# Two weight chunks of expert 1 fetched during the output projection, and 32 KB runs from expert 4 on instead of from expert 7

## The chip, the core and the metric

The kernel runs on one NeuronCore of one Trainium2 chip. The metric is the device time of one execution, in microseconds; the kernel before was run three times and gave 1279.51, 1280.52 and 1283.01 us, median 1280.52 us. Five engines take part: TensorE (PE) multiplies matrices, VectorE (DVE), ScalarE (ACT) and GpSimd (POOL) do element-wise work, and SyncE (SP) issues the transfers from HBM into the on-chip memory (SBUF), which 16 DMA engines then carry.

## The reference: what is computed

One decoder layer over 256 tokens of width 1024, all in float32. The input is layer-normalised, then a token mixer runs: one combined projection `x @ w_in` feeds a gated delta-rule branch, a short-convolution branch and a cross-attention branch; each is projected by `w_br` and gated, the three are summed, and `merged @ w_o` is the output projection. After a second layer norm comes a mixture of experts:

```python
logits = x @ w_router + b_router          # 32 experts, each token takes its top 4
gu = xb @ w_gate_up[e] + b_gate_up[e]     # 1024 -> 2048 for the tokens of expert e
gate, up = split(gu); gate = min(gate, 7); up = clip(up, -7, 7)
h = (up + 1.0) * (gate * sigmoid(gate * 1.702))
y += (h @ w_down[e] + b_down[e]) * weight # 1024 -> 1024
```

and a last layer norm. Every expert has 8 MB of `w_gate_up` and 4 MB of `w_down`, so the 32 experts together read 384 MB (402.7 million bytes), each byte once.

## The kernel before, in words

**Mixer.** The mixer's weights come in 21 pieces of 2 MB through three buffers (`raw`). Each is split into a high and a low part (ACT casts, DVE or POOL subtracts), and PE makes three products per matmul from them. The last two pieces are the two halves of `w_o`. The left operands live in `src_hi`/`src_lo` (branch outputs) and `act_hi`/`act_lo` (the normalised input, later the merged sum). PE needs `src` until the last branch projection `("br", 0, 7)`, and `act` until the last output projection `("wo", 1, 1)`. DVE's eight `sum` steps (line 1623) follow the last branch projections; `wait_sums(eng, KD)` waits for the last of them.

**Experts.** An item is one expert with up to 64 of its tokens; there are 32 items here. Its weights are six chunks of 2 MB: chunks 0 to 3 hold `w_gate_up`, chunks 4 and 5 `w_down`. This text numbers the chunks of all experts in one row: chunk m is part m % 6 of expert m // 6, so expert 1 has chunks 6 to 11, expert 4 begins with chunk 24 and expert 7 with chunk 42. PE works through them in order. After the quarters q = 0, 1, 2 of gate/up it raises `chunks_used`, after q = 3 `gu_done`, after the first half of the down projection `chunks_used`, after the second `down_done`.

**The ring.** The chunks land in a ring of ten slots of 2 MB, and an eleventh slot, `once`, takes chunk 10 only. Chunk m has slot m for m < 10, slot (m - 1) % 10 for the chunks after chunk 10, and slot m % 10 from `PAIRED_FROM` on (`slot_of`). At that place one slot is skipped. SP issues the transfers in order. Before it issues one, it waits until PE has used up what lies in the slot (`chunk_spent`). All chunks are on one DMA queue of SP. The memory of the ring's slots 0 to 5 is free early (slots 0 to 2 once the mixer's weights have been split), the slots 6 to 9 (`late_slots`) lie over the mixer's `act`/`src` tensors, and in slot 9 lies also `x1T`, the transposed input of the router, which PE needs until the four `residual` steps have raised `x1_added`. In `once` lie the router's tables, free when `onehots` has been raised.

**Single and paired transfers.** Before `PAIRED_FROM` each chunk is a transfer of its own, 128 rows with one run of 16 KB each (`chunk_dma`, line 792), and waits for the chunk that used its slot: chunk m waits for chunk m - 10 (m - 11 up to m = 20). From `PAIRED_FROM` on the four gate/up chunks of an expert come as two transfers of 4 MB, with runs of 32 KB into two neighbouring slots (`pair_dma`, line 797), and the waits are other ones: the pair (m, m + 1) waits for chunk m - 8, a down chunk m for chunk m - 9.

Of the kernel before, what the change touches and what calls it, by code (L numbers as in the profile page):

```python
# [29 lines left out]
F32R = mybir.dt.float32r  # L30
# [7 lines left out]
P = 128  # L38
D = 1024
T = 256  # L40
NT = T // P
KD = D // P
# [17 lines left out]
EC = 6  # L60
RING = 10
ROUND = 5
# [106 lines left out]
def hybrid_layer(nc, x, mem, ln0_g, ln0_b, w_in, conv_qkv, conv_mix, a_log, dt_bias, gdn_norm,  # L169
                 w_mem_kv, w_br, w_o, ln1_g, ln1_b, w_router, b_router, w_gate_up, b_gate_up,  # L170
                 w_down, b_down, ln2_g, ln2_b, out):
    with ExitStack() as ctx:
        def sb(name, shape, dt=F32, scope=ctx):
            return scope.enter_context(nc.sbuf_tensor(name, shape, dt))

        def sem(name):
            return ctx.enter_context(nc.semaphore(name))
# [56 lines left out]
        early = ExitStack()  # L234
# [32 lines left out]
        probs = e.at(o_mem, H, 2 * T).rearrange("p h (t m) -> p h t m", t=NT)  # L267
        gates = e.at(o_mem, KD, T)
        GATED = e.used
        act_hi, act_lo = (sb(n, [P, KD, T], F32R, early) for n in ("act_hi", "act_lo"))  # L270
        src_hi, src_lo = (sb(n, [P, KD, T], F32R, early) for n in ("src_hi", "src_lo"))
        s_max, s_neg, s_sum, s_rec = (e.new(H, NT) for _ in range(4))
        w_ab, ab_rows = e.at(o_qkv + R, KD, 2 * H), e.at(o_eb, T)
        chunk_ident = sb("chunk_ident", [P, CHUNK], scope=early)
# [11 lines left out]
        l = Space(sb("late", [P, LATE]), LATE)  # L286
# [14 lines left out]
        cnt, ext, ext2 = l.new(1), l.new(1), l.new(1)  # L301
        assert l.used <= GATED, (l.used, GATED)
        scratch = scratch.rearrange("p a b -> p (a b)")
# [5 lines left out]
        weightT4 = sig1[:, T:T + P]  # L309
        late_slots = [l.new(SLOT) for _ in range(4)]  # L310
        both = l.used - 4 * SLOT
        x1T = l.at(l.used - KD * T, KD, T)


        assert l.used <= LATE - SLOT, (l.used, LATE)
        l.used = LATE - SLOT
        once_o = l.used; once = l.new(SLOT)
        o = once_o
        logits, el, mask = (l.at(o + NT * NE * n, NT, NE) for n in range(3))
        o += 3 * NT * NE  # L320
        top_v, top_f, top_e = (l.at(o + NT * 8 * n, NT, 8) for n in range(3))
# [35 lines left out]
        x1_added = sem("x1_added")  # L357
# [16 lines left out]
        onehots, gathered, tokens_in = sem("onehots"), sem("gathered"), sem("tokens_in")  # L374
# [11 lines left out]
        def bank_of(u):  # L386
            return unit_at[u] % BANKS

        def turn_of(u):
            return unit_at[u] // BANKS + 1  # L390
# [358 lines left out]
        def wait_sums(eng, count):  # L749

            for c in range(max(0, count - BANKS), count):
                eng.wait_ge(bank_free[bank_of(("br", 0, c))], turn_of(("br", 0, c)))
# [25 lines left out]
        def raw_spent(sp, n):  # L778

            for who in split_lo:  # L780
                sp.wait_ge(split_lo[who], lo_count(4 * n + 3, who))


        def chunk_dma(sp, c, gu, dn, dst, landed):


            if c < 4:
                src = gu[4 * P * (c // 2):4 * P * (c // 2 + 1), :].rearrange("(p k) n -> p (k n)", k=4)
                src = src[:, SLOT * (c % 2):SLOT * (c % 2 + 1)]
            else:  # L790
                src = dn[4 * P * (c - 4):4 * P * (c - 3), :].rearrange("(p k) n -> p (k n)", k=4)
            sp.dma_start(dst, src).then_inc(landed, 16)

        def pair_dma(sp, c, gu, m):

            src = gu[4 * P * (c // 2):4 * P * (c // 2 + 1), :].rearrange("(p k) n -> p (k n)", k=4)
            sp.dma_start(PAIRS[slot_of(m) // 2], src).then_inc(ring_place(m)[1], 16)
# [4 lines left out]
        def slot_of(m):  # L802


            return m % RING if m < RING or m >= PAIRED_FROM else RING if m == RING else (m - 1) % RING

        def signals(m):

            return m < PAIRED_FROM or m >= (NE - 1) * EC or m % 2 == 0 or m % EC == EC - 1

        def ring_place(m, rounds=0):

            r = slot_of(m)
            fill = MIXER_FILLS[r] + sum(signals(n) for n in range(m + 1) if slot_of(n) == r)
            per_round = sum(signals(n) for n in range(2 * ROUND * EC, 3 * ROUND * EC) if slot_of(n) == r)
            return RING_SLOTS[r], RING_IN[r], (rounds * per_round + fill) * 16
# [8 lines left out]
        def chunk_spent(eng, m, items=0):  # L825

            i, c = items + m // EC, m % EC
            if c == 3:
                eng.wait_ge(gu_done, i + 1)
            elif c == 5:  # L830
                eng.wait_ge(down_done, i + 1)
            else:
                eng.wait_ge(chunks_used, 4 * i + (c + 1 if c < 3 else 4))

        PAIRED_FROM = (2 + ROUND) * EC
        EARLY_CHUNKS = {15: 3, 16: 4, 17: 5}

        block = ctx.enter_context(nc.Block())  # L840
# [2 lines left out]
        def _(sp):  # L843
# [20 lines left out]
            for n in range(2, N_MIX):  # L864
                slot_dma(sp, n)
                if n in EARLY_CHUNKS:

                    sp.wait_ge(ya_ready, 1)
                    c = EARLY_CHUNKS[n]
# [4 lines left out]
            for r in range(4):  # L874
                n, c = r // 2, r % 2
                sp.dma_start(bgu[NE * r:NE * (r + 1), :], b_gate_up[0, :, FF * n + 512 * c:FF * n + 512 * (c + 1)]).then_inc(ebias_in, 16)
            for n, m in enumerate((ln1_g, ln1_b)):
                for c in range(2):
                    sp.dma_start(gb_cols[:, n, 4 * c:4 * c + 4],
                                 m[0, 4 * P * c:4 * P * (c + 1)].rearrange("(p k) -> p k", k=4)).then_inc(lnp_in[1], 16)  # L880
            for c in range(RAW):
                raw_spent(sp, N_MIX - RAW + (c - N_MIX) % RAW)
                chunk_dma(sp, c, w_gate_up[0, 0], w_down[0, 0], *ring_place(c)[0:2])
            sp.wait_ge(bank_full[bank_of(("wo", 1, 1))], turn_of(("wo", 1, 1)))
            for c in range(EC):
                if EC + c == RING - 1:

                    sp.wait_ge(x1_added, 2 * NT)
                if EC + c == RING:
                    sp.wait_ge(onehots, 1)  # L890
                if EC + c > RING:
                    chunk_spent(sp, EC + c - RING - 1)
                chunk_dma(sp, c, w_gate_up[0, 1], w_down[0, 1], *ring_place(EC + c)[0:2])
            for ex in range(2, 2 + ROUND):
                for c in range(EC):
                    m = EC * ex + c
                    chunk_spent(sp, m - RING - (m <= 2 * RING))
                    chunk_dma(sp, c, w_gate_up[0, ex], w_down[0, ex], *ring_place(m)[0:2])
                if ex == 3:
                    chunk_spent(sp, RING)  # L900
                    for r in range(4):
                        sp.dma_start(bdown[NE * r:NE * (r + 1), :], b_down[0, :, 512 * (r % 2):512 * (r % 2 + 1)]).then_inc(ebias_in, 16)
            with sp.Fori(1, ROUNDS - 1) as j:
                for u in range(ROUND):
                    ex = ROUND * j + (2 + u)
                    gu = w_gate_up[0, bass.ds(ex, 1), :, :].rearrange("e d f -> (e d) f")
                    dn = w_down[0, bass.ds(ex, 1), :, :].rearrange("e d f -> (e d) f")
                    for c in range(0, 4, 2):
                        m = EC * (2 + ROUND + u) + c
                        chunk_spent(sp, m + 2 - RING, ROUND * (j - 1))  # L910
                        pair_dma(sp, c, gu, m)
                    for c in range(4, EC):
                        m = EC * (2 + ROUND + u) + c
# [3 lines left out]
            for ex in range(2 + ROUND * (ROUNDS - 1), NE):  # L917
                paired = ex < NE - 1
                for c in range(EC):
                    m = EC * ex + c  # L920
# [13 lines left out]
            with sp.If_ne(sp.to_reg(n_items), NE):  # L934
                with sp.Fori(NE, n_items) as i:
                    ex = sp.value_load(ids_i[0:1, bass.ds(i, 1)], min_val=0, max_val=NE - 1)
# [255 lines left out]
        def _(pe):  # L1192
# [3 lines left out]
            def piece(q):  # L1196

                pe.wait_ge(split_lo[lo_engine(q)], lo_count(q))
                _, hi, lo = piece_views(q)
                return hi, lo  # L1200
# [716 lines left out]
```

## Time and profile before

| | |
|---|---|
| median of 3 runs | 1280.52 us (1279.51 to 1283.01) |
| time of the profiled execution | 1282.62 us |
| its span | 1280.9 us |
| share of the span: PE / DVE / ACT / POOL busy | 95% / 31% / 19% / 11% |
| HBM read | 451.64 MB |
| experts: first gate/up matmul to last down matmul | 361.16 us to 1266.8 us |

The profile shows one execution. PE's busy share says little by itself, since matmuls are pipelined and their recorded ends are modelled; who is waited for is read from the chain of waits and from the issue and landing times of the transfers. "To landing" is the time from a transfer's issue on SP until all of it is there, so it includes the time it stands in the queue behind earlier ones.

### The profile page before, as it was taken

Reading aid. Unit: us, or ns where it says so; the run is one execution under the profiler, and the core shown is the slowest. Engines: PE = TensorE matmul, PEld = TensorE weight load, DVE = VectorE, ACT = ScalarE, POOL = GpSimd, SP = SyncE. Lnnn points to the kernel's source line nnn. Section 1 sums busy time; section 2 is a strip of 40 time slices with the busy share of each in tenths; the row PEclk is TensorE's granted clock in tenths of the full one; section 3 lists DMA queues with packets and bytes.
Section 4 is the critical chain, followed back from the end, with each engine's and each line's share of the span. In section 5 each row is a group of like instructions: output and inputs, shape, how many; then the busy total and the mean of one; then the engine's idle time right before and its main releaser. Section 6 shows DMA issues by size and latency. Waiting matters only on the chain.

```text
span 1280.9 us, 16880 instructions
## 1 busy us (share of the span) xinstructions
PE 1217.3 (95%) x7135; PEld 616.2 (48%) x7135; DVE 392.6 (31%) x784; ACT 241.3 (19%) x387; POOL 146.1 (11%) x106
## 2 busy tenths in 40 slices
PE   6989999999999999999999999999999999999996
PEld 5789999998843333333333333333333333333332
DVE  5375553434521221221221221221112222122224
ACT  4355345444310000000000000000000000000001
POOL 8223432455200000000000000000000000000000
PEclk9899999999999999999999999999999999999998
DMA  9533323475799999999999999999999999999994
GB/s 299 200 133 132 115 85 128 171 304 196 277 401 420 398 427 426 420 431 428 430 435 428 431 430 427 433 431 427 430 430 430 432 432 426 429 432 430 426 425 179
DMA packets 49512, 453.62 MB, mean 354 GB/s; under 512 B 6110, under 2 KB 10283, under 8 KB 31019
## 3 DMA queue, kind: packets, MB, share of 16 engines
q1 hardware_dynamic: 49450, 452.71, 85.2%
q8 instruction: 51, 0.84, 0.3%
q14 instruction: 11, 0.08, 0.0%
HBM read 451.64 MB, written 1.05 MB: 353 GB/s over the span
## 4 chain that ended last, share of the span: by engine, by line
PE 72%; DMA 19%; DVE 3%; ACT 2%; POOL 2%; issue 1%; SPq 0%; ACTq 0%; DVEq 0%; POOLq 0%
PE bank L1386 27%; DMA late<-in_w_gate_up_dram 19%; PE bank L1459 13%; PE bank L1203 6%; PE bank L1204 5%; PE bank L1205 5%; PE bank L1472 4%; PE bank L1357 3%; PE bank L1372 2%; PE bank L1447 1%; ACT late L1175 1%; POOL w_lo L758 1%; ACT w_hi L1079 1%; PE bank L1467 1%; PE bank L559 1%
## 5 line engine op out<-in xcount | busy, mean ns | idle before, releaser
L1386 PE MATMUL bank<-late 128*64 128x512 f32 x1632 | 368.1, 598 | 10.4 <-DMA late<-in_w_gate_up_dram 10.2
L1386 PEld LDWEIGHTS bank<-late 128*64 128x64 f32 x1632 | 112.6, 137 | 242.2 <-issue 217.6
L1459 PE MATMUL bank<-late 128*64 128x512 f32 x816 | 182.5, 599 | 5.3 <-ACT late L1175 5.3
L1203 PE MATMUL bank<-act_hi,w_hi 128*128 128x256 f32 x448 | 130.1, 290 | 6.9 <-POOL w_lo L758 3.7
L1204 PE MATMUL bank<-act_lo,w_hi 128*128 128x256 f32 x448 | 126.5, 282 | 0.0
L1205 PE MATMUL bank<-act_hi,w_lo 128*128 128x256 f32 x448 | 126.4, 282 | 0.0
L1802 DVE TENSOR_SCALAR late<-bank 128x512 f32<-128x512 f32 x32 | 22.1, 692 | 306.2 <-PE bank L1386 306.1
L1459 PEld LDWEIGHTS bank<-late 128*64 128x64 f32 x816 | 56.9, 138 | 112.8 <-issue 104.4
L1386 PE MATMUL bank<-raw,late 128*64 128x512 f32 x416 | 93.4, 596 | 3.2 <-DMA raw<-in_w_gate_up_dram 3.2
L758 POOL TENSOR_TENSOR w_lo<-raw,w_hi 128x1024 fp32r<-128x1024 f32 x33 | 82.0, 2487 | 117.0 <-ACT w_hi L1079 116.9
L1203 PEld LDWEIGHTS bank<-act_hi,w_hi 128*128 128x128 f32 x448 | 85.1, 190 | 9.3 <-issue 4.1
L1204 PEld LDWEIGHTS bank<-act_lo,w_hi 128*128 128x128 f32 x448 | 85.2, 190 | 0.1
L1205 PEld LDWEIGHTS bank<-act_hi,w_lo 128*128 128x128 f32 x448 | 85.1, 190 | 0.0
L1168 ACT COPY late<-bank 128x512 f32<-128x512 f32 x33 | 19.3, 586 | 331.6 <-PE bank L1357 331.6
L1813 DVE COPY late<-bank 64x512 f32<-64x512 f32 x32 | 22.2, 694 | 189.9 <-PE bank L1459 189.9
L1079 ACT CAST w_hi<-raw 128x1024 fp32r<-128x1024 f32 x56 | 58.5, 1047 | 80.2 <-issue 48.3
L1472 PE MATMUL bank<-late 64*128 64x512 f32 x256 | 63.6, 615 | 1.0 <-DVE late L1873 1.0
L1357 PE MATMUL bank<-hx,late 128*64 128x512 f32 x264 | 62.3, 593 | 0.0
L1177 ACT COPY late<-bank 64x512 f32<-64x512 f32 x32 | 18.5, 579 | 232.0 <-PE bank L1459 232.0
L1386 PEld LDWEIGHTS bank<-raw,late 128*64 128x64 f32 x416 | 28.6, 137 | 62.5 <-issue 55.8
L1173 ACT ACTIVATE late<-late 128x512 f32<-128x512 f32 x32 | 20.1, 629 | 180.4 <-DVE late L1802 180.4
L1817 DVE COPY late<-bank 128x256 f32<-128x256 f32 x31 | 13.2, 425 | 130.3 <-PE bank L1467 130.3
(320 smaller groups left out, 1247.6 us busy)
## 6 DMA issues: line engine op xcount, KB each, us to landing
late<-in_w_gate_up_dram SPq DMA_DIRECT2D x38, 4096.0 KB, 31.8
late<-in_w_down_dram SPq DMA_DIRECT2D x51, 2048.0 KB, 30.6
late<-in_w_gate_up_dram SPq DMA_DIRECT2D x26, 2048.0 KB, 13.5
raw<-in_w_gate_up_dram SPq DMA_DIRECT2D x10, 4096.0 KB, 31.7
raw<-in_w_down_dram SPq DMA_DIRECT2D x13, 2048.0 KB, 32.9
raw<-in_w_in_dram SPq DMA_DIRECT2D x8, 2048.0 KB, 7.8
early<-in_w_in_dram SPq DMA_DIRECT2D x6, 2048.0 KB, 7.6
raw<-in_w_gate_up_dram SPq DMA_DIRECT2D x6, 2048.0 KB, 10.6
```

The lines of the kernel that those rows point to most:

```text
L758: ops.tensor_tensor(lo, src, as_f32(hi), ALU.subtract).then_inc(split_lo[who], 1)
L1079: a.copy(hi, src).then_inc(split_hi, 1)
L1203: mm(o, l_hi, r_hi, start=start, stop=False)
L1204: mm(o, l_hi, r_lo, start=False, stop=False)
L1205: return mm(o, l_lo, r_hi, start=False, stop=stop)
L1357: ins = mm(ps[0][64 * c:64 * c + 64, :], onehot[:, t, :], hx[:, t, 512 * c:512 * (c + 1)], start=(t == 0), stop=(t == NT - 1))
L1372: mm(ps[1 + n][64 * c:64 * c + 64, :], e_row[rows, :], bgu[rows, :], start=True, stop=False)
L1386: ins = mm(bk[64 * c:64 * c + 64, :], x_slotT[:, k % 4, 64 * (k // 4):64 * (k // 4) + 64], w[:, kk, at + 512 * c:at + 512 * (c + 1)], star ...
L1459: ins = mm(ps[3][64 * c:64 * c + 64, :], hidT[:, kk, 64 * q:64 * q + 64], w[:, kk, c * 512:(c + 1) * 512], start=(q == 0 and kk == 0), sto ...
L1472: ins = mm(ps[4 + 2 * t + c][:, :], scatter[64 * c:64 * c + 64, t * P:(t + 1) * P], y_tok[64 * c:64 * c + 64, :], start=False, stop=True, ...
L1802: d.tensor_scalar(gate1, ps[1][:, :], LIMIT, None, ALU.min).then_inc(gate_cut, 1)
L1813: d.tensor_copy(y_tok[64:128, :], ps[3][64:128, :]).then_inc(y_copied, 1)
```

## The change

Four edits. (1) `src_hi`/`src_lo` and `act_hi`/`act_lo` change places in memory, so that the ring's slots 6 and 7 lie over `src` alone. (2) `x1T` moves from slot 9 into `once`. (3) The chunks 6 and 7 are issued between the chunks 0 and 1, after the wait for the mixer's last sum. The chunks 8 and 9 stay behind the last output projection (9 no longer waits for `x1_added`), and chunk 10 waits for `x1_added` and `onehots`. (4) `PAIRED_FROM` goes from 42 to 24.

```diff
+        src_hi, src_lo = (sb(n, [P, KD, T], F32R, early) for n in ("src_hi", "src_lo"))
         act_hi, act_lo = (sb(n, [P, KD, T], F32R, early) for n in ("act_hi", "act_lo"))
-        src_hi, src_lo = (sb(n, [P, KD, T], F32R, early) for n in ("src_hi", "src_lo"))
...
-        x1T = l.at(l.used - KD * T, KD, T)
...
+        x1T = l.at(once_o + 1024, KD, T)
...
-        PAIRED_FROM = (2 + ROUND) * EC
+        PAIRED_FROM = 4 * EC
...
+            def second(c):
+                chunk_dma(sp, c, w_gate_up[0, 1], w_down[0, 1], *ring_place(EC + c)[0:2])
+
             for c in range(RAW):
                 raw_spent(sp, N_MIX - RAW + (c - N_MIX) % RAW)
                 chunk_dma(sp, c, w_gate_up[0, 0], w_down[0, 0], *ring_place(c)[0:2])
+                if c == 0:
+
+                    wait_sums(sp, KD)
+                    second(0)
+                    second(1)
             sp.wait_ge(bank_full[bank_of(("wo", 1, 1))], turn_of(("wo", 1, 1)))
-            for c in range(EC):
-                if EC + c == RING - 1:
-
-                    sp.wait_ge(x1_added, 2 * NT)
-                if EC + c == RING:
-                    sp.wait_ge(onehots, 1)
-                if EC + c > RING:
-                    chunk_spent(sp, EC + c - RING - 1)
-                chunk_dma(sp, c, w_gate_up[0, 1], w_down[0, 1], *ring_place(EC + c)[0:2])
+            second(2)
+            second(3)
+            sp.wait_ge(x1_added, 2 * NT)
+            sp.wait_ge(onehots, 1)
+            second(4)
+            chunk_spent(sp, 0)
+            second(5)
             for ex in range(2, 2 + ROUND):
                 for c in range(EC):
                     m = EC * ex + c
-                    chunk_spent(sp, m - RING - (m <= 2 * RING))
-                    chunk_dma(sp, c, w_gate_up[0, ex], w_down[0, ex], *ring_place(m)[0:2])
+                    if m < PAIRED_FROM:
+                        chunk_spent(sp, m - RING - (m <= 2 * RING))
+                    elif c >= 4 or c % 2 == 0:
+                        chunk_spent(sp, m + (1 if c >= 4 else 2) - RING)
+                    if m >= PAIRED_FROM and c < 4:
+                        if c % 2 == 0:
+                            pair_dma(sp, c, w_gate_up[0, ex], m)
+                    else:
+                        chunk_dma(sp, c, w_gate_up[0, ex], w_down[0, ex], *ring_place(m)[0:2])
```

The order of SP's transfers at the first place, between the mixer and the first expert. The name in brackets is the semaphore waited for; `128x4096` is a chunk of 2 MB. Before, the rows are chunks 0 and 1, 2, 6, 7 and 8, 9, 10, 11:

```order
L792 DMA raw<-in_w_gate_up_dram 128x4096 [waits split_lo_pool,split_lo_dve] x2
L792 DMA late<-in_w_gate_up_dram 128x4096 [waits split_lo_pool,split_lo_dve]
L792 DMA late<-in_w_gate_up_dram 128x4096 [waits bank_full0]
L792 DMA late<-in_w_gate_up_dram 128x4096 x2
L792 DMA late<-in_w_gate_up_dram 128x4096 [waits x1_added]
L792 DMA late<-in_w_down_dram 128x4096 [waits onehots]
L792 DMA raw<-in_w_down_dram 128x4096 [waits chunks_used]
```

And in the changed kernel, chunks 0, 6, 7, 1, 2, 8, 9, 10, 11:

```order
L792 DMA raw<-in_w_gate_up_dram 128x4096 [waits split_lo_pool,split_lo_dve]
L792 DMA late<-in_w_gate_up_dram 128x4096 [waits bank_free2,bank_free1,bank_free0]
L792 DMA late<-in_w_gate_up_dram 128x4096
L792 DMA raw<-in_w_gate_up_dram 128x4096 [waits split_lo_pool,split_lo_dve]
L792 DMA late<-in_w_gate_up_dram 128x4096 [waits split_lo_pool,split_lo_dve]
L792 DMA late<-in_w_gate_up_dram 128x4096 [waits bank_full0]
L792 DMA late<-in_w_gate_up_dram 128x4096
L792 DMA late<-in_w_down_dram 128x4096 [waits onehots,x1_added]
L792 DMA raw<-in_w_down_dram 128x4096 [waits chunks_used]
```

The chunks 6 and 7 have moved from behind `bank_full0` to the place behind chunk 0, and chunk 9 has lost its wait for `x1_added`.

The second place on SP is the end of expert 3 and expert 4. Before: chunk 23 (`w_down`), the four `b_down` pieces, then the chunks 24 to 29:

```order
L792 DMA late<-in_w_down_dram 128x4096 [waits chunks_used]
L902 DMA late<-in_b_down_dram 32x512 [waits chunks_used]
L902 DMA late<-in_b_down_dram 32x512 x3
L792 DMA late<-in_w_gate_up_dram 128x4096 [waits chunks_used]
L792 DMA late<-in_w_gate_up_dram 128x4096 [waits gu_done]
L792 DMA late<-in_w_gate_up_dram 128x4096 [waits chunks_used]
L792 DMA late<-in_w_gate_up_dram 128x4096 [waits down_done]
L792 DMA late<-in_w_down_dram 128x4096 [waits chunks_used] x2
```

In the changed kernel, the same stretch; `128x8192` is a pair of 4 MB:

```order
L792 DMA late<-in_w_down_dram 128x4096 [waits chunks_used]
L915 DMA late<-in_b_down_dram 32x512 [waits chunks_used]
L915 DMA late<-in_b_down_dram 32x512 x3
L797 DMA late<-in_w_gate_up_dram 128x8192 [waits chunks_used] x2
L792 DMA late<-in_w_down_dram 128x4096 [waits chunks_used] x2
```

Four single transfers have become two pairs. The first pair's `chunks_used` is that of chunk 16 (the first half of item 2's down projection), where chunk 24 by itself waited for chunk 14 (the third quarter of its gate/up). PE, DVE, ACT and POOL carry out the same instructions in the same order as before.

## Rows read from the trace of the kernel before

**Rows 1.** The page: busy shares, and the span in 40 slices.

```profile
PE 1217.3 (95%) x7135; PEld 616.2 (48%) x7135; DVE 392.6 (31%) x784; ACT 241.3 (19%) x387; POOL 146.1 (11%) x106
GB/s 299 200 133 132 115 85 128 171 304 196 277 401 420 398 427 426 420 431 428 430 435 428 431 430 427 433 431 427 430 430 430 432 432 426 429 432 430 426 425 179
```

**Rows 2.** The chain that ended last: start us, us, what.

```profile
426.45 6.87 PE bank L1386 x32
453.96 6.87 PE bank L1386 x32
...
784.24 6.87 PE bank L1386 x32
...
806.35 33.59 DMA late<-in_w_gate_up_dram
839.99 7.09 PE bank L1386 x32
...
1186.12 35.58 DMA late<-in_w_gate_up_dram
```

**Rows 3.** Stages: window, length, busy us of PE, PEld, DVE, ACT, POOL, clock, DMA share, GB/s.

```profile
320.00:340.00 20.00, 19.90 (x86) 15.66 (x84) 8.74 (x12) 6.82 (x7) 9.45 (x12) 1.00 0.54 204
340.00:360.00 20.00, 19.26 (x146) 17.48 (x146) 13.73 (x55) 6.27 (x17) 0.00 (x0) 0.91 0.95 384
442.00:526.00 84.00, 83.43 (x398) 28.38 (x394) 18.81 (x39) 7.14 (x12) 0.00 (x0) 1.00 1.00 425
520.00:540.00 20.00, 20.00 (x98) 6.42 (x96) 2.44 (x7) 1.17 (x2) 0.00 (x0) 1.00 0.99 417
537.00:980.00 443.00, 432.05 (x2052) 147.33 (x2048) 99.40 (x205) 37.62 (x64) 0.00 (x0) 1.00 1.00 430
```

**Rows 4.** Timeline of SP, issues of chunks 0, 1, 9, 10 and 11.

```profile
309.69 0.33 SPq L792 DMA_DIRECT2D raw<-in_w_gate_up_dram  x1
322.72 0.33 SPq L792 DMA_DIRECT2D raw<-in_w_gate_up_dram  x1
354.95 0.33 SPq L792 DMA_DIRECT2D late<-in_w_gate_up_dram  x1
355.32 0.43 SPq L792 DMA_DIRECT2D late<-in_w_down_dram  x1
364.78 0.33 SPq L792 DMA_DIRECT2D raw<-in_w_down_dram  x1
```

**Rows 5.** Issue to landing (last number, us): chunk 1, chunk 11.

```profile
raw<-in_w_gate_up_dram SPq DMA_DIRECT2D x1, 2048.0 KB, 7.3
raw<-in_w_down_dram SPq DMA_DIRECT2D x1, 2048.0 KB, 10.6
```

**Rows 6.** Timeline of DVE, the mixer's last sum.

```profile
318.97 0.42 DVE L1623 TENSOR_TENSOR act_lo<-bank,act_hi 128x256 fp32r<-128x256 f32 x1 [0.45 <-ACT act_hi L1146]
```

**Rows 7.** Timeline of SP, issues of chunks 23, 25, 26, 32, and pair 42.

```profile
424.77 0.33 SPq L792 DMA_DIRECT2D late<-in_w_down_dram  x1
433.36 0.35 SPq L792 DMA_DIRECT2D late<-in_w_gate_up_dram  x1
440.30 0.33 SPq L792 DMA_DIRECT2D late<-in_w_gate_up_dram  x1
467.81 0.33 SPq L792 DMA_DIRECT2D raw<-in_w_gate_up_dram  x1
523.01 0.35 SPq L797 DMA_DIRECT2D late<-in_w_gate_up_dram  x1
```

**Rows 8.** Issue to landing of chunks 21, 23, 25, and of pair 42.

```profile
raw<-in_w_gate_up_dram SPq DMA_DIRECT2D x1, 2048.0 KB, 9.2
late<-in_w_down_dram SPq DMA_DIRECT2D x1, 2048.0 KB, 11.6
late<-in_w_gate_up_dram SPq DMA_DIRECT2D x1, 2048.0 KB, 13.7
late<-in_w_gate_up_dram SPq DMA_DIRECT2D x1, 4096.0 KB, 13.5
```

## The prediction

> **What bounds the kernel now.** I read the page first. PE is busy for 95% of the span, and from the 12th of the 40 slices on the core reads 400 to 435 GB/s in every slice up to the last [rows 1]. Both could be the bound, so the chain of waits comes next. Up to 784 us it is PE alone: the same step of an item comes at 453.96 and, twelve items later, at 784.24, which is 330.28 / 12 = 27.52 us an item [rows 2]. From 806 us on the chain runs through transfers: a pair issued at 806.35 lands 33.6 us later and PE starts on it at once; the last such step is the pair issued at 1186.12, landed at 1221.7. What follows it is PE at its own pace and the tail.
>
> Why it changes over: the stage table gives 430 GB/s at a DMA share of 1.00 from 537 to 980 us [rows 3]. A chunk has 2.097 MB, so it takes 4.877 us and an item 29.3 us. The transfers are 1.7 us an item slower than PE. The ring holds more than an item and a half of lead, PE eats it up over some sixteen items, and from there the DMA engines set the time. In the end the time is **when the DMA queue's last bytes land**. Everything that keeps the queue from moving bytes, anywhere between the first chunk and the last, moves the end by as much, and everything that moves bytes into idle time brings it forward, as long as the queue does not run dry in between. So the question for each edit is: where does the queue idle, before and after?
>
> **Where it idles before.** In 320 to 340 us the share is 0.54 (204 GB/s), then 0.95 [rows 3]: this is the hole into which the chunks 6 and 7 are put. The queue's backlog is read from landings: a lone chunk lands 7.3 us after its issue [rows 5], that is 4.9 us of transfer and 2.4 us around it. Chunk 11, issued at 364.78, lands 10.6 us later at 375.4 [rows 4, 5]: only 3.3 us of backlog. Chunk 21 takes 9.2 us, a backlog of 1.9, the least of all; chunk 23 takes 11.6 us, and chunk 25 takes 13.7 us, landing at 433.36 + 13.7 = 447.1 [rows 7, 8]. The second hole is at the change to pairs: pair 42 is issued at 523.01 and lands at 536.5 [rows 7, 8], and in 520 to 540 the rate is 417 instead of 430 GB/s [rows 3], (430 - 417) x 20 / 430 = 0.6 us. From there to the end I see no hole.
>
> **The early fetch.** The mixer's last sum ends at 318.97 + 0.42 = 319.4 us [rows 6], so the chunks 6 and 7 go out at 319.5, three us before chunk 1 (322.72 [rows 4]). They land at about 327 and 332, chunk 1 behind them at about 337 instead of 330.0, chunk 2 at about 342. The first item needs them only at 361 us, so that costs nothing. Bytes moved ahead of the old schedule: 2 x 4.877 = 9.8 us. But the chunks behind are bound by other things. Chunks 8 and 9 (free at 340) are in by about 353; chunk 10 still waits for `x1_added` and the one-hots, 354.95 [rows 4], and lands at 362.3 at the earliest; chunk 11 still waits for item 0's first quarter, 364.78 [rows 4], and lands at 364.78 + 7.3 = 372.1 at the earliest, 3.3 us sooner than before. The queue has idled 6.5 us in between. So of 9.8 us at most 3.3 us are carried over, the backlog that chunk 11 had, and chunk 21 with its 1.9 us lets only that much past: **1.9 us of the 9.8 are left**. With single transfers chunk 25 would land at 445.2 instead of 447.1.
>
> Moving `x1T` and swapping `src` and `act` cost nothing: same instructions on PE, DVE and ACT, only other addresses. Chunk 9 without `x1_added` gains nothing by itself, since chunk 10 waits for it right behind. No wait is added in front of mixer work: on SP behind the `wait_sums` stands only chunk 1, whose own wait ends 3.3 us later.
>
> **Pairs from expert 4 on.** This removes 6 of 18 issues on SP (0.33 us each [rows 7], beside running transfers: nothing) and changes the waits, and here lies the price. Chunk 24 waited for chunk 14 and chunk 25 for 15 (433.36). As a pair they wait for chunk 16, the same that chunk 26 waited for, so the pair goes out at **440.30** [rows 7]. By then the queue is empty: chunk 23 has landed at 424.77 + 11.6 = 436.4 before [rows 7, 8], and now 1.9 us sooner, with only `b_down` behind it (four pieces of 64 KB, about 1 us). Before, chunks 24 and 25 were under way in that time. This also wipes out what the early fetch brought, whatever its size: where the queue runs empty, it does not matter how early it did.
>
> When does the pair land? Lower bound: a lone chunk's 7.3 us plus a second chunk's 4.9 us, 12.2 us. Upper bound: 13.5 us, what pair 42 took with the end of chunk 41 still ahead of it [rows 8]. I take the middle, 12.9, since pair 42 stood behind something and a lone pair does not: 440.30 + 12.9 = 453.2 us, against 447.1 for chunk 25 before: 6.1 us late.
>
> Does the queue run dry again in experts 4 to 6? The next pairs wait for chunks 18, 22, 24 and so on. Pair 30 is closest: it waits for chunk 22, as chunk 32 did, 467.81 [rows 7]; chunk 29 would land at 453.2 + 4 x 4.88 = 472.7, so with a lone pair's 12.2 to 13.5 us the pair could land at 481.3 at the latest and by its turn lands at 482.5. No new hole, by 1.2 us. The later pairs have more, since PE gains 1.7 us per item on the queue.
>
> From chunk 25 to chunk 43 are 18 chunks. At the paired rate, 18 x 4.877 = 87.8 us: chunk 43 lands at 453.2 + 87.8 = **541.0 us**. Before: 536.5. The 1.6 us less than the 6.1 are the 32 KB runs (425 against 430 GB/s [rows 3]: 0.057 us a chunk, 1.0 us in all) and the second hole, which goes away because the skipped slot is now behind us. **Sum: +4.5 us.** From chunk 43 on the queue is full in both kernels, and the shift stays to the end: PE, later by nothing at 541 (it needs the pair at about 555), begins to wait for transfers 4.5 / 1.8 = 2.5 items earlier and waits 4.5 us more in all.
>
> The Trainium skill speaks for the pairs: Perfetto Trace Analysis, DMA Optimizations, says that larger DMAs saturate HBM better. The same list says that smaller transfers may let some of them start sooner, and that speaks against this change. The rows show both, with sizes: 0.057 us a chunk for the one, and 6 us at the first pair for the other. DMA: Bandwidth & Descriptors (Where 436 GB/s comes from) gives a ceiling of 435 GB/s; an estimate by it for 18 chunks is 86.8 us instead of 87.8, a sum lower by 1 us.
>
> In the profiled execution's terms 1282.62 + 4.5 = 1287.1 us; the median of before is 2.1 us lower than that execution, and I put the same shift on it: 1280.52 + 4.5 = **1285.0 us**. With the two bounds of the first pair the shift is 3.8 to 5.1 us; the three runs of before are 3.5 us apart, so the forecast's own range is 1282.5 to 1287.5.
>
> **Rivals.**
> - *The early fetch survives* (the first pair finds enough backlog, or the lost time is made up by better pairs): then the carried 1.9 us and no loss, 1278.6 us. For it speaks that the hole at 320 to 340 is real. Against it: at 440.30 there must be bytes in the queue, and chunk 23 landed at 436.4 before.
> - *All 9.8 us count*, because the backlogs of the chunks 11 and 21 are more than I read: 1270.7 us. Against it: two waits of PE work (354.95, 364.78) that the change leaves alone.
> - *No change*: the pairs win as much as the hole costs, or the end hangs on something else. For a shift of 0 the 18 chunks would have to be 4.5 / 18 = 0.25 us faster each, four times what the two rates show. The time would be 1280.5.
> - *A pair into an empty queue costs more than any pair seen* (on the slower side): no 4 MB transfer of before starts into an empty queue. It decides from 13.5 us after issue on; if 32 KB runs double also the 2.4 us around a lone chunk's transfer and the ramp before it, at 15 us, chunk 25 lands at 455.3 and chunk 43 at 543.1: +6.6 us, 1287.1 us. For it: pair 42 has 3.7 us beyond its 9.8 of transfer, a chunk only 2.4. Against it: part of those 3.7 is chunk 41's end.
>
> **How the numbers follow.** Within 0.3%, 3.8 us, a difference can't be told from none here. Forecast 0.70, early fetch survives 0.13, all of it 0.04, no change 0.08, the costly pair 0.05. The forecast's 4.5 us lie just over the bound of 3.8, so three tenths of its chance fall to "same": slower 0.70 x 0.7 + 0.05 = 0.54; faster 0.04 + three tenths of 0.13 = 0.08; same 0.38. The range from 1279.5 to 1288 takes in the no-change case and the costly pair; it leaves out the full gain, two thirds of the early-fetch case (0.09) and 0.06 of the forecast's own far ends.
>
> **What would show it in the profile after.** Chunks 6 and 7 issued near 319.5, and 320 to 340 us near 400 GB/s. Chunk 10 landing near 362, chunk 11 near 372, a thin stretch between 353 and 366. The first 4 MB transfer issued at 440.3, and some 7 us with next to no bytes before 442; its landing near 453. The pair of expert 7 landing near 541. PE's first wait for a transfer near 770 us instead of 840. The last such step ending near 1226 instead of 1221.7. Wrong would be: bytes flowing at full rate from 434 to 442 us, or chunk 43 landing before 538 us; or an end that does not move with chunk 43.

## The result and the profile after

Over 20 runs each, the changed kernel took 1286.82 us (median; 1284.36 to 1289.62) and the kernel before 1282.49 us (1279.01 to 1286.37). The ratio is 1.0031 with a 95% interval of 1.0022 to 1.0039: **slower by 4.3 us** by the medians, where 4.5 had been forecast. The three runs that were shown before had a median 2 us below that of the 20, so the predicted 1285.0 us lies 1.8 us under the measured time; the shift is the better number to compare.

The page of the changed kernel, the lines that answer to [rows 1]:

```profile
PE 1215.6 (95%) x7135; PEld 614.6 (48%) x7135; DVE 392.6 (31%) x784; ACT 241.0 (19%) x387; POOL 146.2 (11%) x106
GB/s 298 201 132 132 132 68 132 213 299 188 359 331 418 315 433 426 435 425 429 430 430 435 428 431 431 429 430 430 428 430 432 430 429 434 427 431 431 427 427 181
```

The slices 11 and 12 together have hardly more than before (277 and 401), and the 14th has only 315 GB/s, where it had 398. Stage by stage (columns as in [rows 3]):

```profile
320.00:340.00 20.00, 19.58 (x97) 15.96 (x96) 10.01 (x16) 6.87 (x10) 8.29 (x11) 1.00 0.99 411
340.00:360.00 20.00, 19.59 (x134) 16.70 (x134) 11.45 (x50) 5.17 (x14) 0.00 (x0) 0.83 0.70 282
434.00:442.00 8.00, 8.00 (x42) 2.42 (x40) 1.96 (x5) 0.58 (x1) 0.00 (x0) 1.00 0.54 197
520.00:540.00 20.00, 20.00 (x98) 6.28 (x94) 2.74 (x7) 1.73 (x3) 0.00 (x0) 1.00 1.02 435
541.00:980.00 439.00, 424.00 (x2012) 144.14 (x2010) 97.81 (x203) 36.83 (x62) 0.00 (x0) 1.00 1.00 430
```

The early chunks fill the stretch from 320 to 340 (0.54 before, 0.99 now), but the next one falls from 0.95 to 0.70: the bytes were moved, and the queue then had nothing to do. From 434 to 442 it moved bytes for half of the time. At 520 to 540 the hole of before is gone. The rate of the long stage is the same 430 GB/s.

The single transfers, as SP issued them: chunk 0, chunk 10, chunk 11, the first pair (24, 25) and pair 42.

```profile
306.70 0.33 SPq L792 DMA_DIRECT2D raw<-in_w_gate_up_dram  x1
353.50 0.33 SPq L792 DMA_DIRECT2D late<-in_w_down_dram  x1
363.34 0.33 SPq L792 DMA_DIRECT2D raw<-in_w_down_dram  x1
437.32 0.35 SPq L797 DMA_DIRECT2D late<-in_w_gate_up_dram  x1
520.03 0.35 SPq L797 DMA_DIRECT2D late<-in_w_gate_up_dram  x1
```

Of these, pair 42 took, from issue to landing:

```profile
late<-in_w_gate_up_dram SPq DMA_DIRECT2D x1, 4096.0 KB, 18.5
```

The pair (24, 25) took 13.5 us, so it landed at 450.8, and chunk 43 at 538.5. In this execution the mixer was 3.0 us quicker than in that of before (chunk 0 goes out at 306.70 and not at 309.69; in 40 to 60 us the granted clock was 1.00 and not 0.93 and 0.90), and the first item had a deeper dip of the clock (0.83 in 340 to 360, 0.91 before). So times are compared from an anchor: the issue that waits for chunk 16, the first half of item 2's down projection. Before, that is chunk 26 at 440.30 [rows 7]; in the changed kernel it is the first pair at 437.32. From the anchor, chunk 43 landed after 96.2 us before [rows 7, 8] and 101.2 us now: **5.0 us later**. The chain of the changed kernel, as in [rows 2], with PE's last down projection as its last line:

```profile
708.82 7.09 PE bank L1472 x32
...
720.69 33.55 DMA late<-in_w_gate_up_dram
754.25 0.04 issue
...
1188.40 35.18 DMA late<-in_w_gate_up_dram
...
1261.58 7.11 PE bank L1472 x32
```

and the same step before:

```profile
1259.70 7.11 PE bank L1459 x32
```

On this chain PE first waits for a transfer at 754 us instead of about 840, and its last down projection starts 1261.58 - 437.32 = 824.3 us after the anchor. Before, it started 1259.70 - 440.30 = 819.4 us after it: now 4.9 us later. The shift of chunk 43 has gone through to the end, undiminished, over 720 us.

### The profile page after: what moved, and what is told of

Its sections match the earlier page's. It is cut to its first block, busy times and chain, and to the rows that moved or that the text cites. A ratio compares the mean times of both kernels' runs of the same rounds, so it can differ in the third digit from the quotient of the medians.

```text
span 1282.7 us, 16879 instructions
## 1 busy us (share of the span) xinstructions
PE 1215.6 (95%) x7135; PEld 614.6 (48%) x7135; DVE 392.6 (31%) x784; ACT 241.0 (19%) x387; POOL 146.2 (11%) x106
## 4 chain that ended last, share of the span: by engine, by line
PE 67%; DMA 25%; DVE 3%; ACT 2%; POOL 2%; issue 1%; SPq 0%; ACTq 0%; DVEq 0%; POOLq 0%
DMA late<-in_w_gate_up_dram 24%; PE bank L1399 24%; PE bank L1472 12%; PE bank L1216 6%; PE bank L1217 5%; PE bank L1218 5%; PE bank L1485 3%; PE bank L1370 3%; PE bank L1385 2%; PE bank L1460 1%; ACT late L1188 1%; POOL w_lo L758 1%; ACT w_hi L1092 1%; PE bank L559 1%; PE bank L1253 0%
## 5 line engine op out<-in xcount | busy, mean ns | idle before, releaser
L1399 PE MATMUL bank<-late 128*64 128x512 f32 x1632 | 366.4, 596 | 13.4 <-DMA late<-in_w_gate_up_dram 13.3
```

The source lines that it names most:

```text
L1399: ins = mm(bk[64 * c:64 * c + 64, :], x_slotT[:, k % 4, 64 * (k // 4):64 * (k // 4) + 64], w[:, kk, at + 512 * c:at + 512 * (c + 1)], star ...
```

## The experiments

The theory: the time is set by when the DMA queue's last bytes land. The pair rule lets the queue run dry in front of expert 4 (loss 5 us), and whatever the early fetch gained before that is wiped out there. The rivals are told with each kernel. Each was timed beside the kernel before (pairs_only 6 times, the others 11 or 12 times, the kernel before 23 or 35 times). The table has the traces by the anchor (us after the issue that waits for chunk 16; in brackets the difference to before) and the timed ratio with its 95% interval.

| kernel | anchor | chunk 43 landed | last down starts | ratio |
|---|---|---|---|---|
| before | 440.30 | 96.2 | 819.4 | 1 |
| changed | 437.32 | 101.2 (+5.0) | 824.3 (+4.9) | 1.0031 (1.0022 to 1.0039) |
| early_only | 438.72 | 96.3 (+0.1) | 819.2 (-0.2) | 1.0001 (0.9990 to 1.0012) |
| pairs_only | 441.38 | 101.4 (+5.2) | 824.4 (+5.0) | 1.0042 (1.0026 to 1.0059) |
| slots24 | 439.02 | 96.7 (+0.5) | 819.8 (+0.4) | 1.0002 (0.9990 to 1.0014) |
| after_30 | 438.58 | 99.7 (+3.5) | 822.5 (+3.1) | 1.0025 (1.0016 to 1.0035) |
| after_36 | 441.47 | 97.8 (+1.6) | 820.9 (+1.5) | 1.0003 (0.9992 to 1.0015) |
| early_from54 | 441.78 | 94.7 (-1.5) | 818.8 (-0.6) | 0.9998 (0.9986 to 1.0009) |
| late_from54 | 440.23 | 95.8 (-0.4) | 819.5 (+0.1) | 1.0002 (0.9989 to 1.0015) |

How far two traces differ by chance can be seen here too: late_from54 and the kernel before issue the same transfers up to chunk 41, and yet it landed 86.0 us after the anchor in the one and 85.3 in the other. Differences of up to some 0.6 us between single traces show nothing by themselves.

### The early fetch alone

```diff
-        PAIRED_FROM = 4 * EC
+        PAIRED_FROM = 7 * EC
```

> Chunks 6 and 7 early as in the changed kernel, pairs from expert 7 on as before. My theory: the queue runs thin at chunk 21 (1.9 us of backlog) and is refilled at pair 42 by that pair's own issue, so nothing is left of the 9.8 us: the transfer that brings chunk 43 lands 226.8 us after the issue of chunk 0, as before, and the time is that of before within 0.5 us. Rival (the early bytes are carried to the end, the pairs alone are to blame): chunk 43 lands 224.9 us or less after chunk 0's issue, and the time is 1.9 to 3.3 us below before; at the full 9.8 us, 217.0 us.

Measured: 1282.24 us against 1282.67, ratio 1.0001. Chunk 0 went out at 308.22. SP's timeline has pair 42 at

```profile
521.44 0.35 SPq L797 DMA_DIRECT2D late<-in_w_gate_up_dram  x1
```

and from issue to landing it took (last number)

```profile
late<-in_w_gate_up_dram SPq DMA_DIRECT2D x1, 4096.0 KB, 13.6
```

521.44 + 13.6 - 308.22 = 226.8 us, the expected number, while chunk 41 had landed at 523.3. So nothing of 9.8 us is left at chunk 43. The interval ends at 0.9990, 1.3 us below before, so the rival's smallest gain of 1.9 us is out. How much was carried up to there is read from two places. Chunk 11 landed 7.6 us after its issue in the changed kernel (10.6 before [rows 5]): 3.0 us carried, 3.3 reckoned. Chunk 21, issued at 414.64, took

```profile
raw<-in_w_gate_up_dram SPq DMA_DIRECT2D x1, 2048.0 KB, 8.6
```

8.6 us (the same in the changed kernel) and not the 7.3 of a lone chunk, where it took 9.2 before [rows 8]. So 0.6 us get past it, not 1.9; chunk 25 landed 6.0 us after the anchor against 6.7 before, 0.7 us. Most had been lost earlier, at a place that the prediction did not look at: against the kernel before, by the anchor, chunk 15 landed 2.6 us ahead, the chunks 16 to 20 1.1 us, and chunk 21 0.6 us.

### The pairs alone

The kernel before, its old layout and order, with the changed kernel's branch for the pairs in SP's loop and

```diff
-        PAIRED_FROM = (2 + ROUND) * EC
+        PAIRED_FROM = 4 * EC
```

> The layout and the order of the first twelve chunks as before, pairs from expert 4 on. My theory: the first pair's issue (130.6 us after chunk 0's) sets everything behind it, whether the queue before it was early or not, so chunk 43 lands 231.8 us after chunk 0's issue, as in the changed kernel, and the time is 4.3 to 5.0 us above before. Rival (the early fetch softens or causes part of the loss): 233.7 us and 6.5 us above before if the 1.9 us of the early fetch were kept in the changed kernel; less than 3 us above before if the early fetch itself did harm.

Measured: 1287.89 us against 1282.67, ratio 1.0042, 5.4 us. From chunk 0's issue chunk 43 took 233.3 us, more than the 231.8 expected and near the rival's 233.7. That reading is spoilt by the clock: it was 0.94 in 309 to 340 us here, and the first item began 1.3 us later. By the anchor (the clock is 1.00 from there to chunk 43 in all these kernels) chunk 43 is 5.2 us late, as in the changed kernel (5.0), and the last down projection 5.0 (4.9). The transfers:

```profile
441.38 0.35 SPq L797 DMA_DIRECT2D late<-in_w_gate_up_dram  x1
524.09 0.35 SPq L797 DMA_DIRECT2D late<-in_w_gate_up_dram  x1
```

The first pair landed after 13.3 us, pair 42 after 18.7. The intervals of the two ratios overlap over most of their length. The interval here goes from 3.3 to 7.6 us and takes in the rival's 6.5, so a help of the early fetch of some 2 us is not excluded by the timing, only by the traces (0.2 us).

### One slot less, but single transfers

```diff
         PAIRED_FROM = 4 * EC
+        PAIR_DMA_FROM = 7 * EC
...
-                    elif c >= 4 or c % 2 == 0:
-                        chunk_spent(sp, m + (1 if c >= 4 else 2) - RING)
-                    if m >= PAIRED_FROM and c < 4:
+                    elif c >= 4 or c % 2 == 0 or m < PAIR_DMA_FROM:
+                        chunk_spent(sp, m + (1 if c >= 4 or m < PAIR_DMA_FROM else 2) - RING)
+                    if m >= PAIR_DMA_FROM and c < 4:
```

and the count of landings (`signals`) goes by `PAIR_DMA_FROM`.

> The changed kernel with the paired numbering of the slots from chunk 24 on (one slot is skipped there, and each chunk m waits for chunk m - 9), but with single transfers of 2 MB and a wait for each up to chunk 41; pairs from chunk 42. My theory: the price is the pair's late issue (both halves wait for the later of two slots). With single transfers chunk 24 goes out 123.7 us after chunk 0 instead of 130.6, no stretch without bytes is longer than 2 us, chunk 43 lands 226.8 to 227.2 us after chunk 0's issue and the time is that of before within 0.7 us. Rival (the skipped slot, so one chunk less of lead, is the price): chunk 43 lands near 231 us and the time is 4 us above before.

Measured: 1282.75 us, ratio 1.0002. SP's timeline, the chunks 24 and 25:

```profile
432.08 0.35 SPq L792 DMA_DIRECT2D late<-in_w_gate_up_dram  x1
439.02 0.35 SPq L792 DMA_DIRECT2D late<-in_w_gate_up_dram  x1
```

From issue to landing, in the same order:

```profile
late<-in_w_gate_up_dram SPq DMA_DIRECT2D x1, 2048.0 KB, 7.5
...
late<-in_w_gate_up_dram SPq DMA_DIRECT2D x1, 2048.0 KB, 7.3
```

Chunk 25 goes out at the same event as the changed kernel's first pair, but by then chunk 24 is just landing (439.6), and 25 lands at 446.3, 7.3 us after the anchor, where the pair took 13.5. The stretch around it, in this kernel and then in the changed one:

```profile
430.00:442.00 12.00, 11.81 (x58) 4.37 (x54) 4.22 (x7) 1.22 (x2) 0.00 (x0) 1.00 0.85 303
```

```profile
430.00:442.00 12.00, 11.80 (x60) 4.34 (x60) 4.64 (x9) 1.18 (x3) 0.00 (x0) 1.00 0.47 164
```

The difference, 139 GB/s over 12 us, is 1.7 MB or 3.9 us at 430 GB/s: so much queue time the changed kernel lets go by in this stretch alone. Skipping the slot at chunk 24 and not at chunk 42 costs 0.5 us by the trace and nothing that the timing shows (1.8 us at most). The 0.5 is a net sum: at chunk 41 slots24 is 2.4 us behind early_only, which differs from it only in where the slot is skipped (87.0 and 84.6 us after the anchor), and from chunk 41 to chunk 43 it wins 2.0 back (9.7 us against 11.7).

The remaining 4.5 us of the changed kernel come with the pairs: in the main with holding chunk 24 back for chunk 25's slot. What the 4 MB transfer by itself adds to that was not tested by a run with two single transfers issued together at the anchor. The nearest rows are the chunks 6 and 7 of the changed kernel, which go out together when the queue has been empty since 313.97:

```profile
316.51 0.80 SPq L792 DMA_DIRECT2D late<-in_w_gate_up_dram  x2
late<-in_w_gate_up_dram SPq DMA_DIRECT2D x1, 2048.0 KB, 7.6
late<-in_w_gate_up_dram SPq DMA_DIRECT2D x1, 2048.0 KB, 12.2
```

Chunk 7, issued at 316.88, landed at 329.0, 12.5 us after the first issue (12.5 to 12.9 in the six kernels with the early fetch), where the pairs took 13.3 to 13.8. So up to some 1 us of the 4.5 can belong to the form of the transfer and not to the wait.

### The change to pairs one and two experts later

`PAIRED_FROM = 5 * EC` and `6 * EC` in the changed kernel.

> The changed kernel with pairs from expert 5 (chunk 30) instead of expert 4. My theory: each item that the change to pairs comes later gives the queue 1.7 us more to live on, so the hole shrinks. Pair 30 goes out 158.1 us after chunk 0 into an empty or nearly empty queue, lands 13.4 us later, and chunk 43 lands 230.0 us after chunk 0's issue (226.8 before, 231.8 changed): the time is 3.2 us above before. Rival (the hole does not depend on the place): as the changed kernel, 4.3 us or more above before.

> The same with pairs from expert 6 (chunk 36). My theory: pair 36 goes out 185.6 us after chunk 0, lands at 199.0, chunk 43 lands at 228.3, and the time is 1.5 us above before. Rival (place does not matter): 4.3 us above.

Measured: 1286.14 us, ratio 1.0025 (3.2 us), and 1283.84 us, ratio 1.0003 (0.4 us, at most 1.9; the medians are 1.2 apart). The first pair's issue in each; they landed after 13.8 and 13.4 us:

```profile
466.09 0.33 SPq L797 DMA_DIRECT2D raw<-in_w_gate_up_dram  x1
```

```profile
496.50 0.33 SPq L797 DMA_DIRECT2D late<-in_w_gate_up_dram  x1
```

By the anchor the end is late by 4.9, 3.1 and 1.5 us for a change at experts 4, 5 and 6, and early by 0.2 us at expert 7 (early_only): about 1.7 us for each, which is what PE gains on the queue in an item. The rival (place does not matter) is out for expert 6 by the timing too; for expert 5 the interval goes up to 4.5 us and takes in the rival's 4.3, so there it is out by the trace alone (chunk 43 3.5 us late and not 5.0). In after_36 pair 36 went out 186.9 us after chunk 0 and not 185.6, since the first item again began late; the anchor takes that out.

### The change to pairs only when the queue is deep

`PAIRED_FROM = 9 * EC`, with the unrolled part of SP's loop going on to expert 11 (`range(2, 2 + 2 * ROUND)`, the loop from 2), once with the early fetch and once without.

> Early fetch as in the changed kernel, single transfers up to expert 8, pairs from expert 9 on (chunk 54). My theory: by chunk 54 the queue holds so much that the change to pairs leaves no hole. The 1.9 us of the early fetch are then carried, and the hole of 1.2 us at chunk 42 goes away, against 0.3 to 0.7 us for the slower single transfers of experts 7 and 8: 2.4 us below before. The pair of chunk 55 lands 282.7 us after chunk 0's issue, 285.3 before. Rival (32 KB runs are worth more than 0.06 us a chunk): the same time as before or above it.

> The kernel before (no early fetch, old layout) with pairs from expert 9 on. My theory: only the hole at chunk 42 goes, chunk 55 lands 284.6 us after chunk 0's issue, and the time is 0.7 us below before; the early fetch is then worth 1.9 us more when nothing behind it empties the queue. Rival (the early fetch is worthless in any case): the same time as the kernel with the early fetch and pairs from expert 9.

Measured: 1283.04 us, ratio 0.9998 (0.9986 to 1.0009), and 1282.69 us, ratio 1.0002. **The first misses**: 2.4 us were forecast, and the interval ends at 1.8. The hole did go away: with the early fetch chunk 53 was issued at 563.81 and landed at 585.5, and pair 54, issued at 579.33, landed 9.7 us behind it:

```profile
563.81 0.33 SPq L792 DMA_DIRECT2D late<-in_w_down_dram  x1
579.33 0.33 SPq L797 DMA_DIRECT2D late<-in_w_gate_up_dram  x1
```

The pair's time to landing:

```profile
late<-in_w_gate_up_dram SPq DMA_DIRECT2D x1, 4096.0 KB, 15.8
```

But chunk 55 came 153.4 us after the anchor, 1.3 us sooner than before (154.7) and not 2.6, since only 0.6 us of the early fetch had got past chunk 21 here (chunk 25 landed 6.2 us after the anchor, 6.7 before). The gain lasts until chunk 179, still 1.3 us ahead; the twelve chunks of the last two experts then took 59.1 us against 58.6, and at the last down projection 0.6 us are left. Why those twelve differ is open (58.6 to 59.7 us in the nine traces). Without the early fetch, chunk 55 came at 154.9, 0.2 us later than before, where 0.7 sooner was expected; 0.6 us of that miss was there at chunk 41 already, before the two kernels differ. So the early fetch is worth 1.5 us at chunk 55 and 0.6 to 0.7 at the end by two traces, little more than two traces differ by chance, and nothing that the timing can show. No kernel here beats the one before.

## Why the prediction was right

**What bounds the kernel.** Right, and shown: in the eight kernels beside that of before the last down projection moved by what chunk 43 moved by, within 0.5 us in seven and 0.9 in one (early_from54).

**The early fetch.** The mechanism held: issued behind the last sum (chunk 6 at 316.51, 9.8 us after chunk 0, as reckoned), bytes moved into the hole (0.54 to 0.99), then idle again until chunks 10 and 11 could go. Its size was off: "1.9 us of the 9.8 are left" are 0.6 to 0.7. The failing piece is the lone chunk's 7.3 us as a lower bound: chunk 21 took 8.5 to 8.6 us in the six kernels with the early fetch, issued 2.1 to 3.2 us before chunk 20 had landed, and chunk 15 8.1 to 8.9. It is no rule for every chunk at such a place (chunk 24 of slots24, issued 2.1 us before the last landing, took 7.5), and its cause is open. For the changed kernel it made no difference, since the first pair resets it; it is a term that spoilt the forecast for early_from54.

**The first pair.** Its issue at the anchor and the empty queue came as reckoned: 197 GB/s from 434 to 442 us, and only 164 from 430 to 442. The landing was 13.5 us after issue, the upper of the two bounds, not the middle of 12.9: 0.6 us too little. Against chunk 25 of before (6.7 us after the anchor) it is 6.7 us late, where 6.1 were reckoned. The sum was 4.5 us, the trace has 5.0, the timing 4.3 (0.22% and 0.39% are 2.8 and 5.0 us).

**No second hole.** Pair 30, the closest, went out at 464.83 and landed at 480.0, 9.7 us behind chunk 29 (470.3): by its turn. The rate of the pairs: 538.5 - 450.8 = 87.7 us for 18 chunks, 87.8 reckoned. Against the 89.5 us of before that wins 1.8 us back, 1.6 reckoned, but the two parts of the 1.6 were both wrong and their errors cancel, which is luck. The second hole was worth 1.3 us and not 0.6: from chunk 41 to chunk 43 it took 10.9 us before and 9.6 now. The 32 KB runs were worth 0.5 us and not 1.0: chunk 25 to chunk 41 took 78.6 us before and 78.1 now, 0.03 us a chunk and not 0.057. That size is near the scatter. In early_from54 the twelve single chunks from 41 to 53 took 58.8 us, 4.90 each, in late_from54 59.2, 4.93 each; the twelve chunks from 43 to 55 in the other seven kernels, eight of them in pairs, took 4.87 to 4.90 each.

**The rivals.** That the early fetch survives is excluded by early_only; that all of it counts, too; that there is no change, by the 20 runs (1.0022 at the least); a pair at 15 us or more, by 13.3 to 13.8 in four kernels (in after_36 the queue ran empty only 0.2 us after the issue). Of the signs named, PE's first wait came at 754 us (770 named), and the last transfer step ended 786.3 us after the anchor, 4.9 us later than before (781.4).

## What to carry to other kernels

When a transfer queue is the bound, count where it stands empty; a prefetch was worth at most the smallest backlog that the queue had anywhere behind it (here 0.6 to 0.7 of 9.8 us), and a later stall reset it to nothing. Merging two transfers makes the first half wait for the second half's buffer, so do it where the queue already holds more than one such transfer, and not at the start, where the ring is only just ahead. To compare traces of a few tenths of a per cent, take times from an event behind the last dip of the clock, not from the start of the span, and look at how far two kernels differ before the place where their code does.

## What was not expected of the hardware

A 4 MB transfer into an empty queue took 13.3 to 13.8 us here, two single 2 MB transfers issued together into an empty queue 12.5 to 12.9 us. Behind a nearly drained queue it was more: in the kernel before, the chunks 6 and 7, issued at 339.94 and 340.32 when chunk 2 was about to land (341.39), landed 7.3 and 13.0 us later:

```profile
late<-in_w_gate_up_dram SPq DMA_DIRECT2D x1, 2048.0 KB, 13.0
```

that is 353.3, or 13.4 us after the first issue. The second 2 MB need 6.1 us there, where in a full queue each needs 4.9; the third (chunk 8, 358.2) again needs 4.9. In the changed kernel chunk 7 landed 4.9 us behind chunk 6 (329.0 and 324.2), so the extra 1.2 us is not a price of every restart, and no run shows what it depends on.

The 32 KB runs were worth about 0.03 us a chunk against 16 KB ones, 0.6% of the transfer time. The Trainium skill (Perfetto Trace Analysis, DMA Optimizations) says that larger DMAs saturate HBM better, and explains it with transfers of a few KB; the measured sizes agree in sign. The same list's remark that smaller transfers let some start sooner weighed more than ten times as much in this place: by the anchor the first pair landed 6.7 us later than chunk 25 before, against 0.5 us for the runs of 32 KB up to chunk 41.
